# Attention: rotating seven query blocks without a TensorE product

## The chip, the cores and the metric

The kernel runs on one core of a Trainium2 chip. The metric is the device time of one launch in microseconds (us). The kernel before takes 3042.12 us, the median of three runs (3040.42 to 3044.2). TensorE is called PE below, VectorE DVE, ScalarE ACT, GpSimd POOL and SyncE SP, as in the profile.

## The reference

One step of a denoising trunk in four layers, for 128 context tokens and 256 latent tokens of width 1024, all in float32. Each layer is a half-step SwiGLU FFN, a mixer and another FFN. The mixer is attention in layers 0 and 3, a short convolution in layer 1, and a bidirectional gated scan in layer 2. Only attention is touched here. It has 16 query heads and 4 key heads of 64 dimensions. The queries and keys of the 256 latent tokens are rotated (axial rope), those of the context tokens are not:

```python
def apply_rope(x, cos, sin):
    x1, x2 = jnp.split(x, 2, axis=-1)      # 32 + 32 of the 64 dimensions of a head
    c = cos[None, :, None, :]
    s = sin[None, :, None, :]
    return jnp.concatenate([x1 * c - x2 * s, x1 * s + x2 * c], axis=-1).astype(x.dtype)

q = apply_rope(q, cos, sin)
k = apply_rope(k, cos, sin)
...
s_lat = jnp.einsum('bnqkgd,bnskd->bnkgqs', qb, kb) * ATTN_SCALE      # masked window
s_ctx = jnp.einsum('bnqkgd,bskd->bnkgqs', qb, k_ctx) * ATTN_SCALE    # cached keys
p = jax.nn.softmax(jnp.concatenate([s_lat, s_ctx, sink_logits], axis=-1), axis=-1)
o = p_latent @ v + p_ctx @ v_ctx
```

## The kernel before

Everything is one program with an instruction order written out by hand for each engine, and semaphores between the engines. Activations are kept transposed: feature on the partition, the 384 tokens (128 context, 256 latent) along the free axis. A weight block is 128x1024. ACT splits it into a high part `w_hi` (L1876) and DVE makes the low part `w_lo` (L2032); this pair is called split(b). PE multiplies a block in 24 products (`in_block`, L1629 to L1631: high by high, high by low, low by high, for eight slices of the model width) into one PSUM bank.

The attention stage (`pe_attn`, `act_attn`, `dve_attn`, `gp_attn`) projects twelve blocks of 128 outputs: two of keys, two of values, and eight of queries. A query block holds two heads: partitions 0 to 63 and 64 to 127. Within a head, dimension m and dimension m xor 32 form a rotated pair, so rotating a block needs the block itself and a copy in which the four runs of 32 partitions ("quarters") are swapped in pairs: 0 with 1, and 2 with 3. The rotated block is block x cosine + swapped block x sine, with the sine table holding the minus sign for quarters 0 and 2.

The order is `ROPE_ORDER`: key blocks 0 and 1, query block 0, key blocks 2 and 3, then query blocks 1 to 7. The first five (`FIRST_ROPES`) are rotated ahead of the loop. The loop has seven steps, j = 0 to 6. In step j,

- PE: `in_block` of query block j+1 into bank 7; `turn_probs(2j-2)` (L611, seven transposes of the probabilities of a head; `turn_values` instead in step 0); `rotate` (L577), which is the swap, done as a product with a permutation matrix into bank 7 again; `values(j-2)` from step 2 on (L629, L636); `turn_probs(2j-1)` from step 1 on; `scores(j+1)` (L592 to L600) of the block just rotated.
- ACT: `probs(2j)` (L725, L727, the exponentials), `take` (L692, bank 7 to `qkv`), `copy_probs(2j-2)` (L714, L716), `probs(2j+1)`, `output(j-2)` (L732, L733), its part of `copy_probs(2j-1)` (L714), the high part of a split.
- DVE: `maxima(2j)` and `maxima(2j+1)` (L796, L800), `normalize(2j)` (L811, L813 and three instructions at L817), `rope` (L780, swapped block x sine, PSUM to `rope_tmp`; L784, the sum), `split(b0+10+j)` (L2032), `copy_probs(2j-1)` (L806), `normalize(2j+1)`.
- POOL: `cosine` (L859, block x cosine in place), which waits for `rope_rot`, PE's signal behind the rotation; `low_part(j-2)` (L863), which waits for `output(j-2)`.

`scores(j+1)` waits for `rope_add`, the signal of the sum at L784. Behind the loop `out_part` multiplies the outputs by the last eight weight blocks, and the first of these waits for `score_read`, the end of the last maxima. The stage is run twice, in layers 0 and 3.

## Time and profile before

| what | value |
| --- | --- |
| median of three runs | 3042.12 us (3040.42 to 3044.2) |
| profiled execution: its time | 3044.6 us |
| profiled execution: its span | 3042.7 us |
| mean granted TensorE clock | 0.994 |
| PE busy | 2970.3 us (98%) |
| DVE busy | 2210.9 us (73%) |
| ACT busy | 1154.8 us (38%) |
| POOL busy | 588.7 us (19%) |
| the two loops over steps | 372.9 to 440.6 us and 2642.7 to 2710.3 us |

The span is from the first to the last instruction. The time of an execution has 1.9 us more around it. Busy time is the sum over an engine's instructions. An instruction that waits inside for a resource counts as busy, so a duration that is longer than that of its like is a sign of waiting. Rows of the timeline give the start from the beginning of the span, the duration (of several merged instructions: from the first start to the last end), and in brackets the idle time before it and what ended it. Two instructions of one engine can overlap in such rows by some 0.1 us.

### The profile page before, as it was taken

The page shows a single profiled execution, that of the slowest core. Times are in us where ns is not written, and L with a number is a line of the kernel's source. Part 1 is how long each engine was busy: PE and PEld are TensorE (multiplying, and loading weights), DVE is VectorE, ACT ScalarE, POOL GpSimd, SP SyncE. Part 2 cuts the span into 40 slices and gives each one's busy share as a digit, 9 for nine tenths or more (in the row PEclk, how much of TensorE's full clock was granted, in tenths as well). Part 3 has the DMA queues.
Part 4 walks back from the last instruction along what each step waited for, and adds up shares of the span by engine and source line. Part 5 has one row for each costly group of instructions (what it writes and reads, how often), then busy time and mean ns, then how long its engine had stood idle before and what let it go on. Part 6 is the DMA issues. An engine that isn't in the chain of part 4 may idle for free.

```text
span 3042.7 us, 46662 instructions
## 1 busy us (share of the span) xinstructions
PE 2970.3 (98%) x18382; PEld 2753.6 (90%) x18382; DVE 2210.9 (73%) x2845; ACT 1154.8 (38%) x1967; POOL 588.7 (19%) x586
## 2 busy tenths in 40 slices
PE   6999999999999999999999999999999999999999
PEld 6989888999999998999899989979999999889998
DVE  5888687877887566888887576668888888775444
ACT  4222575222422434322422265543224222664222
POOL 1111212112211202112211144441112112211001
PEclk9999999999999999999999999999999999999999
DMA  8676535666566354766566533337664766334443
GB/s 295 200 223 194 144 69 174 209 213 206 167 211 189 105 151 140 235 208 196 184 210 203 149 109 98 98 95 235 208 212 155 222 211 201 113 78 121 125 125 97
DMA packets 565935, 515.59 MB, mean 169 GB/s; under 512 B 43014, under 2 KB 499287, under 8 KB 563927
## 3 DMA queue, kind: packets, MB, share of 16 engines
q1 hardware_dynamic: 565158, 512.37, 55.6%
q8 instruction: 147, 2.41, 0.3%
q14 instruction: 70, 0.57, 0.1%
q10 hardware_dynamic: 560, 0.25, 0.0%
HBM read 509.31 MB, written 3.24 MB: 168 GB/s over the span
## 4 chain that ended last, share of the span: by engine, by line
PE 85%; issue 4%; DVE 4%; DMA 3%; ACT 1%; POOL 1%; SPq 1%; another core or an unknown queue 0%; DVEq 0%; POOLq 0%; ACTq 0%
PE bank L1629 18%; PE bank L1631 18%; PE bank L1630 18%; PE bank L1676 8%; PE bank L1678 8%; PE bank L1677 8%; DMA raw<-w_ffn_in 2%; PE bank L1646 2%; PE bank L1653 1%; DVE fold L2054 1%; PE bank L611 1%; DMA raw<-w_ffn_out 1%; PE bank L636 1%; PE bank L1709 1%; POOL small L2300 0%
## 5 line engine op out<-in xcount | busy, mean ns | idle before, releaser
L1629 PE MATMUL bank<-h_hi,w_hi 128*128 128x384 f32 x3328 | 1122.2, 337 | 6.4 <-DVE tmp L2084 4.1
L1631 PE MATMUL bank<-h_hi,w_lo 128*128 128x384 f32 x3328 | 1115.8, 335 | 0.0
L1630 PE MATMUL bank<-h_lo,w_hi 128*128 128x384 f32 x3328 | 1114.6, 335 | 0.0
L1876 ACT ACTIVATE w_hi<-raw 128x1024 fp32r<-128x1024 f32 x648 | 682.8, 1062 | 1090.6 <-PE bank L1631 443.0
L2032 DVE TENSOR_TENSOR w_lo<-raw,w_hi 128x1024 fp32r<-128x1024 f32 x648 | 812.5, 1276 | 346.7 <-ACT w_hi L1876 340.1
L2054 DVE SCALAR_TENSOR_TENSOR fold<-ada_raw,cond,fold 128x1024 f32<-128x1024 f32 x476 | 654.5, 1432 | 0.0
L1629 PEld LDWEIGHTS bank<-h_hi,w_hi 128*128 128x128 f32 x3328 | 626.2, 188 | 18.2 <-DVE tmp L2084 4.4
L1630 PEld LDWEIGHTS bank<-h_lo,w_hi 128*128 128x128 f32 x3328 | 626.2, 188 | 6.0
L1631 PEld LDWEIGHTS bank<-h_hi,w_lo 128*128 128x128 f32 x3328 | 625.9, 188 | 0.0
L2341 POOL TENSOR_TENSOR h_lo<-tmp,h_hi 128x384 fp32r<-128x384 f32 x176 | 280.5, 1594 | 1762.9 <-DVE h_hi L2088 1762.9
L1676 PE MATMUL bank<-w_hi,h_hi 128*128 128x512 f32 x1056 | 416.2, 394 | 0.0
L1678 PE MATMUL bank<-w_hi,h_lo 128*128 128x512 f32 x1056 | 414.1, 392 | 0.0
L1677 PE MATMUL bank<-w_lo,h_hi 128*128 128x512 f32 x1056 | 413.6, 392 | 0.0
L1895 ACT ACTIVATE tmp<-bank 128x384 f32<-128x384 f32 x176 | 86.3, 490 | 442.7 <-PE bank L1631 437.7
L2084 DVE TENSOR_TENSOR tmp<-bank,tmp 128x384 f32<-128x384 f32 x176 | 97.7, 555 | 212.1 <-PE bank L1631 210.2
L1678 PEld LDWEIGHTS bank<-w_hi,h_lo 128*128 128x128 f32 x1056 | 198.4, 188 | 42.4
L1676 PEld LDWEIGHTS bank<-w_hi,h_hi 128*128 128x128 f32 x1056 | 198.7, 188 | 38.6
L1677 PEld LDWEIGHTS bank<-w_lo,h_hi 128*128 128x128 f32 x1056 | 198.7, 188 | 38.1
L1952 ACT ACTIVATE hf<-bank,mod,s_cols 128x128 f32<-128x128 f32 x288 | 106.5, 466 | 27.2 <-PE bank L1709 26.7
L2126 DVE TENSOR_TENSOR og<-bank,g_rows 128x512 f32<-128x512 f32 x72 | 49.3, 684 | 52.6 <-ACT tmp L1929 52.6
L1676 PE MATMUL bank<-w_hi,o_hi 128*128 128x512 f32 x192 | 77.6, 404 | 1.9 <-DVE soft L796 1.0
L2061 DVE TRANSPOSE_TENSOR_REDUCE fold_sums<-fold 128x64 f32<-128x2048 f32 x34 | 78.3, 2304 | 0.0
(199 smaller groups left out, 2411.6 us busy)
## 6 DMA issues: line engine op xcount, KB each, us to landing
raw<-w_ffn_in SPq DMA_DIRECT2D x352, 512.0 KB, 5.0
ada_raw<-w_ada SPq DMA_DIRECT2D x272, 512.0 KB, 4.2
raw<-w_ffn_out SPq DMA_DIRECT2D x176, 512.0 KB, 4.6
raw<-w_hgrn_in SPq DMA_DIRECT2D x40, 512.0 KB, 3.9
g_rows<-g_dram SPq DMA_DIRECT2D x12, 1024.0 KB, 6.8
raw<-w_attn_qkv SPq DMA_DIRECT2D x24, 512.0 KB, 6.1
raw<-w_conv_in SPq DMA_DIRECT2D x24, 512.0 KB, 5.0
ada_first<-w_ada SPq DMA_DIRECT2D x16, 512.0 KB, 12.3
```

The lines of the kernel that those rows point to most:

```text
L1629: mm(out, wh, h_hi[:, k, :], start=(k == 0), stop=False)
L1630: mm(out, wh, h_lo[:, k, :], start=False, stop=False)
L1631: last = mm(out, wl, h_hi[:, k, :], start=False, stop=(k == DC - 1))
L1676: mm(out, hi[:, tokens(t)], w_hi[:, b % RING, columns(n)], start=opens, stop=False)
L1677: mm(out, hi[:, tokens(t)], w_lo[:, b % RING, columns(n)], start=False, stop=False)
L1678: return mm(out, lo[:, tokens(t)], w_hi[:, b % RING, columns(n)], start=False, stop=closes)
L1876: A(w_hi[:, b % RING, :], raw[:, b % RAW, :], ACT.Copy).then_inc(w_hi_made, 1)
L1952: last = A(hf[:, t, k, :], psum[2 * t + half][:, k % 4 * P:(k % 4 + 1) * P], ACT.Identity, bias=mod[:, 3 * e * DC + k, g:g + 1], scale=s_c ...
L2032: V.tensor_tensor(w_lo[:, b % RING, :], raw[:, b % RAW, :], w_hi[:, b % RING, :].bitcast(F32), ALU.subtract).then_inc(w_lo_made, 1)
L2054: V.scalar_tensor_tensor(out=acc, in0=slab, scalar=c, in1=acc, op0=ALU.mult, op1=ALU.add).then_inc(fold_made, 1)
L2084: V.tensor_tensor(tmp[:, 2 + f % 2, :], psum[7][:, 0:T], tmp[:, f % 2, :], ALU.mult).then_inc(b_read, 1)
L2341: G.tensor_tensor(h2_lo[:, f % H2, :], tmp[:, 2 + f % 2, :], h2_hi[:, f % H2, :].bitcast(F32), ALU.subtract).then_inc(h2_lo_made, 1)
```

## The change

The rotations of query blocks 1 to 7, in the loop, are made without PE. The rotations ahead of the loop stay as they were.

- PE: `rotate` is gone from the steps. PE now also waits, before it overwrites bank 7, for `rope_swapped` of the step before.
- ACT: behind `take`, a new `swap(n)` makes two copies from bank 7 to `rope_tmp`, of 32 partitions and 256 columns each, with a scale of -1: quarter 3 is written to quarter 2, and quarter 2 to quarter 3. It signals `rope_swapped`.
- DVE: `rope` is replaced in the steps by `turned(n)` and `rope_end(n)`. `turned` waits for `rope_swapped` and makes two products with the sine table, again of 32 partitions and 256 columns: bank 7's quarter 1 into quarter 0 of `rope_tmp`, and quarter 0 into quarter 1. Then comes the split, which used to stand behind the sum. Then `rope_end` subtracts `rope_tmp` from the block, 128x256, as soon as the cosine product, both sine products and POOL's sine product are there.
- POOL: `cosine` waits for `qkv_taken` (the end of `take`) in place of `rope_rot`. A new `sine_low` multiplies partitions 64 to 127 of `rope_tmp` by the sine table, in place, once `rope_swapped` and the cosine product are there.
- The counts of `rope_rot` are changed to five for each attention stage.

```diff
--- before.py
+++ after.py
@@ -395,6 +395,7 @@
     ROPE = KVH + DC
 
     attn_in, attn_turned, attn_turn_copied = sem("attn_in"), sem("attn_turned"), sem("attn_turn_copied")
+    rope_swapped, rope_low = sem("rope_swapped"), sem("rope_low")
     rope_rot, k_dup_done, k_dup_copied = sem("rope_rot"), sem("k_dup_done"), sem("k_dup_copied")
     rope_cos, rope_sin, rope_add = sem("rope_cos"), sem("rope_sin"), sem("rope_add")
     sink8_made, score_done, score_read, neg_made = sem("sink8_made"), sem("score_done"), sem("score_read"), sem("neg_made")
@@ -525,6 +526,12 @@
 
         return 6 + n % 2 if n < FIRST_ROPES else 7
 
+    SWAPS = len(ROPE_ORDER) - FIRST_ROPES
+
+    def quarter(q):
+
+        return slice(32 * q, 32 * q + 32)
+
     def rope_dst(n):
         kind, i = ROPE_ORDER[n]
         return kd[:, i, TP:T] if kind == "k" else qkv[:, i, TP:T]
@@ -567,9 +574,7 @@
 
         def rotate(n):
             kind, i = ROPE_ORDER[n]
-            if n >= FIRST_ROPES:
-                pe.wait_ge(qkv_taken, taken + n + 1)
-            elif n >= 2:
+            if n >= 2:
                 pe.wait_ge(rope_sin, ROPE * a + n - 1)
                 if kind == "q":
                     pe.wait_ge(qkv_taken, taken + 3)
@@ -657,13 +662,16 @@
         scores(0)
         for j in range(DC - 1):
 
-            pe.wait_ge(rope_sin, ROPE * a + FIRST_ROPES + j - (1 if j == 0 else 0))
+            if j == 0:
+                pe.wait_ge(rope_sin, ROPE * a + FIRST_ROPES - 1)
+            else:
+                pe.wait_ge(rope_sin, ROPE * a + FIRST_ROPES + j)
+                pe.wait_ge(rope_swapped, SWAPS * a + j)
             in_block(b0 + FIRST_ROPES + j, 7)
             if j == 0:
                 turn_values()
             else:
                 turn_probs(2 * j - 2)
-            rotate(FIRST_ROPES + j)
             if j >= 2:
                 values(j - 2)
             if j >= 1:
@@ -715,6 +723,12 @@
             if h % 2 == 0:
                 A(pt[h % 3][:, 512:KEYS], psum[5][:, 0:KEYS - 512], ACT.Copy).then_inc(pt_copied_v, 1)
 
+        def swap(n):
+            need(act, rope_add, ROPE * a + n - 1)
+            for q in range(2, 4):
+                last = A(rope_tmp[quarter(q), n % 2, :], psum[7][quarter(q ^ 1), TP:T], ACT.Copy, scale=-1.0)
+            last.then_inc(rope_swapped, 1)
+
         def probs(h):
             act.wait_ge(neg_made, HEADS * a + h + 1)
             if h >= 3:
@@ -750,6 +764,7 @@
         for j in range(DC - 1):
             probs(2 * j)
             take(FIRST_ROPES + j)
+            swap(FIRST_ROPES + j)
             if j == 0:
                 copy_values()
             else:
@@ -776,12 +791,27 @@
 
         def rope(n):
 
-            dve.wait_ge(rope_rot, ROPE * a + n + 1)
+            dve.wait_ge(rope_rot, FIRST_ROPES * a + n + 1)
             V.tensor_tensor(rope_tmp[:, n % 2, :], psum[rope_bank(n)][:, 0:TS], sin_t, ALU.mult).then_inc(rope_sin, 1)
 
             dve.wait_ge(rope_cos, ROPE * a + n + 1)
             dve.wait_ge(rope_sin, ROPE * a + n + 1)
             V.tensor_tensor(rope_dst(n), rope_dst(n), rope_tmp[:, n % 2, :], ALU.add).then_inc(rope_add, 1)
+
+        def turned(n):
+
+            dve.wait_ge(rope_swapped, SWAPS * a + n - FIRST_ROPES + 1)
+            for q in range(2):
+                last = V.tensor_tensor(rope_tmp[quarter(q), n % 2, :], psum[7][quarter(q ^ 1), TP:T],
+                                       sin_t[quarter(q ^ 1), :], ALU.mult)
+            last.then_inc(rope_sin, 1)
+
+        def rope_end(n):
+
+            dve.wait_ge(rope_cos, ROPE * a + n + 1)
+            dve.wait_ge(rope_sin, ROPE * a + n + 1)
+            dve.wait_ge(rope_low, SWAPS * a + n - FIRST_ROPES + 1)
+            V.tensor_tensor(rope_dst(n), rope_dst(n), rope_tmp[:, n % 2, :], ALU.subtract).then_inc(rope_add, 1)
 
         def maxima(h):
             n = HEADS * a + h
@@ -831,8 +861,9 @@
             maxima(2 * j)
             maxima(2 * j + 1)
             normalize(2 * j)
-            rope(FIRST_ROPES + j)
+            turned(FIRST_ROPES + j)
             split(b0 + 10 + j)
+            rope_end(FIRST_ROPES + j)
             if j >= 1:
                 copy_probs(2 * j - 1)
             normalize(2 * j + 1)
@@ -853,10 +884,21 @@
         def cosine(n):
             kind, i = ROPE_ORDER[n]
 
-            gp.wait_ge(rope_rot, ROPE * a + n + 1)
+            if n < FIRST_ROPES:
+                gp.wait_ge(rope_rot, FIRST_ROPES * a + n + 1)
+            else:
+                gp.wait_ge(qkv_taken, len(QKV_CHUNKS) * a + n + 1)
             if kind == "k":
                 gp.wait_ge(k_dup_copied, KVH * a + i + 1)
             G.tensor_tensor(rope_dst(n), rope_dst(n), cos_t, ALU.mult).then_inc(rope_cos, 1)
+
+        def sine_low(n):
+
+            gp.wait_ge(rope_swapped, SWAPS * a + n - FIRST_ROPES + 1)
+            gp.wait_ge(rope_cos, ROPE * a + n + 1)
+            low = rope_tmp[HD:P, n % 2, :]
+            G.tensor_tensor(low, low, sin_t[HD:P, :], ALU.mult).then_inc(rope_low, 1)
+            gp.wait_ge(rope_low, SWAPS * a + n - FIRST_ROPES + 1)
 
         def low_part(c):
             gp.wait_ge(mix_hi_made, DC * mi + c + 1)
@@ -870,6 +912,7 @@
         for j in range(DC + 2):
             if j < DC - 1:
                 cosine(FIRST_ROPES + j)
+                sine_low(FIRST_ROPES + j)
             if j >= 2:
                 low_part(j - 2)
```

## Rows read from the trace of the kernel before

**Rows 1.** The page, part 1: busy time, share of the span and instructions.

```profile
PE 2970.3 (98%) x18382; PEld 2753.6 (90%) x18382; DVE 2210.9 (73%) x2845; ACT 1154.8 (38%) x1967; POOL 588.7 (19%) x586
```

**Rows 2.** Busy time of each engine in the second attention stage, by windows.

```profile
2642.00:2716.00 74.00, 71.77 (x620) 64.15 (x618) 63.44 (x210) 52.96 (x153) 10.87 (x13) 1.00 0.27 60
```

**Rows 3.** Timeline of PE: start, duration, engine, line, tiles; in brackets idle before.

```profile
2642.72 0.70 PE L592 MATMUL bank<-kd,qkv 64*128 64x256 f32 x4
...
2651.53 0.70 PE L592 MATMUL bank<-kd,qkv 64*128 64x256 f32 x4 [1.32 <-DVE qkv L784]
...
2660.48 0.70 PE L592 MATMUL bank<-kd,qkv 64*128 64x256 f32 x4
...
2670.45 0.70 PE L592 MATMUL bank<-kd,qkv 64*128 64x256 f32 x4
...
2676.45 0.93 PE L611 MATMUL bank<-base_k,pr 128*128 128x128 f32 x7
2677.22 0.68 PE L577 MATMUL bank<-qkv,attn_k 128*128 128x256 f32 x2
2677.83 0.44 PE L629 MATMUL bank<-pt,vt 128*64 128x128 f32 x4
...
2679.51 0.98 PE L611 MATMUL bank<-base_k,pr 128*128 128x128 f32 x7
2680.42 0.70 PE L592 MATMUL bank<-kd,qkv 64*128 64x256 f32 x4
```

**Rows 4.** Timeline of DVE, from scores(0) to the step of scores(4).

```profile
2644.66 0.62 DVE L796 CUSTOM_DVE_ANT_0 sm<-bank,attn_k,sink 128x384 f32<-128x384 f32 x1 [0.45 <-PE bank L600]
...
2673.14 0.61 DVE L796 CUSTOM_DVE_ANT_0 sm<-bank,attn_k,sink 128x384 f32<-128x384 f32 x1
...
2676.72 0.16 DVE L811 TENSOR_TENSOR soft<-soft 128x3 f32<-128x3 f32 x1 [0.35 <-ACT soft L727]
...
2677.13 0.94 DVE L817 TENSOR_SCALAR pr<-pr,soft 128x384 f32<-128x384 f32 x3
2677.99 0.42 DVE L780 TENSOR_TENSOR rope_tmp<-bank,attn_k 128x256 f32<-128x256 f32 x1
2678.75 0.42 DVE L784 TENSOR_TENSOR qkv<-qkv,rope_tmp 128x256 f32<-128x256 f32 x1 [0.34 <-POOL qkv L859]
2679.09 1.22 DVE L2032 TENSOR_TENSOR w_lo<-raw,w_hi 128x1024 fp32r<-128x1024 f32 x1
2680.53 0.56 DVE L806 COPY pt<-bank 128x384 f32<-128x384 f32 x1 [0.22 <-PE bank L611]
2681.00 1.00 DVE L811 TENSOR_TENSOR soft<-soft 128x3 f32<-128x3 f32 x1
```

**Rows 5.** Timeline of ACT, steps 0 and 3.

```profile
2649.87 0.38 ACT L702 ACTIVATE vt<-bank 128x256 f32<-128x256 f32 x1
...
2676.65 0.49 ACT L692 ACTIVATE qkv<-bank 128x384 f32<-128x384 f32 x1
2677.42 0.60 ACT L714 ACTIVATE pt<-bank 128x512 f32<-128x512 f32 x1 [0.27 <-PE bank L611]
...
2680.42 0.49 ACT L733 ACTIVATE o_hi<-bank 128x384 fp32r<-128x384 f32 x1
```

**Rows 6.** Timeline of POOL, step 3.

```profile
2677.98 0.74 POOL L859 TENSOR_TENSOR qkv<-qkv,attn_k 128x256 f32<-128x256 f32 x1 [5.96 <-PE bank L577]
2680.98 1.00 POOL L863 TENSOR_TENSOR o_lo<-tmp,o_hi 128x384 fp32r<-128x384 f32 x1 [2.27 <-ACT o_hi L733]
```

**Rows 7.** Timeline of DVE before the steps: a split.

```profile
2638.34 1.76 DVE L2032 TENSOR_TENSOR w_lo<-raw,w_hi 128x1024 fp32r<-128x1024 f32 x1
```

**Rows 8.** Timeline of POOL before the steps: a cosine product.

```profile
2638.09 0.92 POOL L859 TENSOR_TENSOR kd<-kd,attn_k 128x256 f32<-128x256 f32 x1
```

**Rows 9.** Timeline of DVE behind the steps: a normalize.

```profile
2717.52 1.77 DVE L817 TENSOR_SCALAR pr<-pr,soft 128x384 f32<-128x384 f32 x3
```

**Rows 10.** Timeline of POOL behind the steps: a low part.

```profile
2717.53 1.02 POOL L863 TENSOR_TENSOR o_lo<-tmp,o_hi 128x384 fp32r<-128x384 f32 x1 [5.63 <-ACT o_hi L733]
```

## The prediction

> **What bounds the kernel now.** I read the page's busy times first: PE is busy for 98% of the span and nothing else comes near [rows 1]. So work taken off PE is worth its time wherever the next engine has room. The windows of an attention stage tell how much room: in 74 us PE is busy for 71.8, but DVE for 63.4 and ACT for 53.0 [rows 2]. DVE is there at 86% of the stage against 73% of the whole kernel. POOL is nearly idle.
>
> Then I read the timeline of the steps. Measured from one start of `scores` to the next, the seven steps take 8.81, 8.95 and five times 9.97 us [rows 3]. Step 3 is the pattern, and I give all its times as offsets from its `scores` at 2670.45. PE has no gap in it: transposes at 6.00, the rotation at 6.77, `values` at 7.38, transposes at 9.06, next `scores` at 9.97 [rows 3]. The rotation holds PE for 7.38 - 6.77 = 0.61 us. Beside it runs a chain: `take` at 6.20 to 6.69 [rows 5], rotation, sine product at 7.54, sum at 8.30 to 8.72 [rows 4]. `scores` needs the sum only at 9.97, so this chain has 1.25 us to spare, less some 0.06 for the signal (in step 0, which has no `values`, PE waits 1.32 us for it [rows 3]). Behind the sum DVE makes its split, from 8.64 on, and the next DVE instruction could start 1.14 us later: 1.22 of duration, less the 0.08 by which the rows of neighbours overlap [rows 4].
>
> **The change, part by part.** *PE.* Seven rotations in each of two stages: 14 x 0.61 = 8.5 us at most, and a full step would last 9.97 - 0.61 = 9.36. The new wait for `rope_swapped` of the step before is long met, since `scores` stands between.
>
> *ACT.* No row shows a copy of 32 partitions. The nearest is the copy of 128x256 from a bank, 0.38 us, 0.26 to its follower's start by my reading of a row's 0.1 us overlap [rows 5]. I take that. The ends are nothing and 0.49 (128x384, [rows 5]). `take` starts at 6.20, the two copies at 6.57 and 6.83, they end at 7.21, and DVE sees it at 7.25. `copy_probs` behind them starts at about 7.09 in place of 6.97 [rows 5], 0.12 late. PE does not notice: it wants that copy at 9.06 less 0.61, and it is made by about 8.1. `output` shifts by the same 0.12, so POOL's low part comes at 10.65 in place of 2680.98 - 2670.45 = 10.53 [rows 6].
>
> *DVE.* The one sine product of 0.42 becomes two, of a quarter of the partitions and the same 256 columns. No row shows such. Ends: nothing and 0.61 (128x384 with a bank, [rows 4]). I take 0.42 each, end to end, 7.25 to 8.09. If they follow at 0.34, as the split follows the sum [rows 4], the second ends at 8.01 and the next can start at 7.93. Then the split, which has changed places with the sum: 8.09 plus 1.14 is 9.23. Then the subtraction, 0.42, as the sum has it: 9.65. With the signal's 0.06, `scores` could start at 9.71, while PE is ready at 9.36. So already without any collision the spare time is used up: the split's 1.14 has been put into a chain with 1.19 to spare, and the second product and the later start take the rest.
>
> The Trainium skill (VectorE: DVE Perf Modes, Two Vector instructions with no wait between them) says that an instruction which starts in another group of 32 partitions than the one before it, for input or output, is held until all earlier ones have finished. No row before shows it. By the rule the products and the split follow at full durations, and by the row at 0.34: the sum below would be 1 to 2 us less by the row.
>
> *POOL.* The cosine no longer waits for PE, so it starts 0.09 behind `take`, at 6.78, in place of 7.53 [rows 6]. `sine_low` has 64 partitions and the cosine's 256 columns. I take the cosine's 0.73 (ends: nothing, and 1.00 for 384 columns [rows 6]). It waits for the cosine's end: 7.59 to 8.32.
>
> *The collision.* A split that is issued while POOL's product runs lasts 1.76 us and not 1.22: it started at 2638.34, POOL's product ended at 2639.01, the split at 2640.10, 1.09 behind that [rows 7, 8]. `normalize` suffers too: with a low part beside it its three instructions took 1.77 us, not 0.94, 0.83 more [rows 4, 9, 10]. So does the small sum at L811, with 1.00 for 0.16 [rows 4, 6]. The sine product from a bank does not: 0.42 with the cosine beside it [rows 4, 6]. So I let a split wait for POOL, and its follower start 1.01 behind POOL's end: 8.32 + 1.01 = 9.33, subtraction to 9.75, `scores` at 9.81.
>
> Steps 0, 1 and 2 come out so, at 9.81: their maxima start 1.94 behind `scores` (step 0, [rows 3, 4]), no low part runs yet, and `normalize(2j)`, which starts 3.99 behind the maxima [rows 4], is over at 6.80. That is +1.00, +0.86 and -0.16 against before.
>
> In steps 3 to 6 the low part, at 10.65, falls 0.84 us into the next step. DVE is then in `normalize` of the odd head, and the maxima start at about 2.4, not 1.94. Before, L811 took the blow and they started at 2.69 [rows 4]. Then `normalize(2j)` runs from 6.39 to 7.25, and the cosine, now at 6.78, falls into its middle. Before, it came at 7.53, behind it. It costs DVE some 0.6 (0.83 for a product of 1.00, scaled to 0.73). The products run from 7.85 to 8.69, the split to 9.83, `scores` starts at 10.31. A step as long as this moves the low part to 0.34 of the next, where it meets either L811 (maxima again at about 2.4) or goes just behind it (at about 2.0, and that step lasts 9.81). I take two in three of the long kind: 10.15, which is +0.18 for each of four steps.
>
> **The sum.** One loop: 1.00 + 0.86 - 0.16 + 4 x 0.18 = 2.4 us. Two loops: 4.8 us. Behind the loop I change nothing. The profiled execution has a span of 3042.7 and a time of 3044.6, so it stands 2.5 us above the median. On its time the sum gives 3049.4, on the median 3046.9, and I forecast 3047. A difference of 0.2%, 6.1 us, is about what a measurement of this kernel can tell from no change, so this is a small loss, just inside it.
>
> **The rivals.**
>
> *No collision costs (20%).* POOL's products slip by DVE or are shorter with 64 partitions. Then steps 0 and 1 end at 9.55 to 9.71, +1.5 for the pair on average, and five steps save 0.42 to 0.26: 1.5 - 1.7 = -0.2 a loop, between -0.8 and +0.4. The time is 3040.5 to 3043. For it: POOL has little to do [rows 2]. Against it: `sine_low` at 7.59 ends where the split begins, by any of my durations.
>
> *Both POOL products cut into `normalize` (16%).* This is the one on the slow side. In steps 3 to 6 DVE's group ends at about 8.75, the split at 10.74, and the low part, due at 10.65, gets in between split and subtraction: `scores` at about 12.1. Such a step leaves the next one clean (9.81), so the mean is 10.95, +0.98 for four steps, 5.6 a loop: 3053. It decides where the maxima start later than about 2.3 and `sine_low` comes before the third instruction of `normalize`.
>
> *PE gets it all back (4%).* That needs the subtraction to end by 9.30, or the products and copies to cost far less on 32 partitions: 3042.1 - 8.5 = 3033.6, less what steps 0 and 1 lose, so some 3036.
>
> *The small instructions are dear (6%).* If each copy takes 0.49 and each product 0.61, a step gets 0.22 + 0.38 = 0.6 longer: 14 x 0.6 = 8.4 on top of 4.8, 3055.
>
> My forecast has 54%.
>
> **How the numbers follow.** My own case reaches from 3044 to 3050. Towards both sides the range takes in the case without collisions (3040.5) and the one in which both products cut in (3053). What is left out is the outer half of the last two rivals and the tails. Faster by over 0.2% (below 3036) is half the third rival and a little of the first: 4%. Slower by over 0.2% (above 3048.2) is 16 + 6, and a fifth of my own case: 33%. Within 0.2%: 63%.
>
> **What would show it.** In the profile after: `scores` about 9.8 us apart in steps 0 and 1 and between 9.8 and 10.4 later; PE waiting for the subtraction ahead of `scores` in each step, 0.4 to 1 us; splits of some 1.4 in the steps; a few `normalize` groups of 1.5; two products of 0.42 behind each other; DVE's busy time up. I am wrong if the rows of 32 partitions are much shorter or longer than those of 128, if `sine_low` ends before DVE's products do, or if the waits of DVE for POOL do not add up along the chain as I let them.

## The result: 0.35% slower

The changed kernel takes 3050.62 us, the median of 8 runs from 3046.66 to 3060.09; the kernel before takes 3040.57 beside it (8 runs, 3037.67 to 3044.98). The ratio is 1.0035, with a 95% interval from 1.0022 to 1.0048, so it is slower by 6.7 to 14.6 us, best 10.6. I had forecast 3047.0 and a range from 3040.5 to 3053.0. The time lies in the range, but it is a loss of more than 0.2%, to which I gave 33%, and it lies just outside my own case of 3044 to 3050. Set on the median that I worked from (3042.12), the ratio gives 3052.8, close to the upper end. The profiled execution took 3051.95 with a span of 3050.1.

The page of the changed kernel, its span and part 1, as in [rows 1]:

```profile
span 3050.1 us, 46690 instructions
...
PE 2965.6 (97%) x18354; PEld 2751.0 (90%) x18354; DVE 2220.9 (73%) x2859; ACT 1165.5 (38%) x1995; POOL 600.9 (20%) x600
```

PE is busy for 4.7 us less, not 8.5. In the seven steps of the first stage, at full clock, it is busy for 62.67 us where it was 65.70; in those of the second it is busy for 67.06 against 65.70, as its products last longer there at a lower clock (below). DVE is busy for 10 more. Then PE's waits in the second attention stage: engine, what it wrote, its line, who released it; total, times, longest.

```profile
PE bank L597 <- DVE qkv L814: 6.3, 6, 3.0
PE bank L616 <- ACT pt L724: 1.7, 1, 1.7
```

Nearly all that PE lost, it lost ahead of `scores`, to the subtraction (L814). One of six waits makes half of the sum. Now the same stage by windows: the 74 us of [rows 2], then step 0, step 1, step 2 and the four steps from 3 to 6 together. Behind each length stand the busy times of PE, PE's weight loads, DVE, ACT and POOL, with the number of instructions; the last three columns are granted clock, DMA share and GB/s.

```profile
2642.00:2716.00 74.00, 66.09 (x516) 59.84 (x516) 61.41 (x197) 51.10 (x146) 14.31 (x18) 0.93 0.27 60
2643.49:2653.51 10.02, 7.05 (x54) 6.58 (x53) 7.79 (x26) 6.73 (x20) 2.17 (x3) 0.96 0.21 65
2653.51:2666.53 13.02, 10.72 (x59) 9.67 (x59) 8.36 (x29) 7.15 (x24) 1.45 (x2) 0.76 0.14 42
2666.53:2678.11 11.58, 11.12 (x87) 9.90 (x87) 8.48 (x30) 7.10 (x22) 1.46 (x2) 0.86 0.15 47
2678.11:2719.19 41.08, 38.17 (x344) 34.84 (x344) 38.46 (x116) 32.45 (x95) 10.42 (x12) 1.00 0.38 58
```

Steps 3 to 6 last 41.08 / 4 = 10.27 each, and step 0 lasts 10.02. Steps 1 and 2 last 13.02 and 11.58, and there the granted clock is 0.76 and 0.86. I had no term for a clock. The other stage shows what these steps are at full clock: its steps last 10.02, 10.00, 10.00, 10.26, 10.26, 10.27 and 10.27, with 1.00 in all. That is 71.08, against 67.63 before, or 3.45 more in a stage; the second stage took 75.70, 4.62 more than the first.

The timeline of PE, second stage, shows what it did before that (start, duration; idle time before in brackets). The rows at the starts of `scores` answer to [rows 3]:

```profile
2653.51 1.23 PE L597 MATMUL bank<-kd,qkv 64*128 64x256 f32 x4 [2.96 <-DVE qkv L814]
...
2664.92 0.96 PE L616 MATMUL bank<-base_k,pr 128*128 128x128 f32 x7 [1.65 <-ACT pt L724]
2666.53 1.22 PE L597 MATMUL bank<-kd,qkv 64*128 64x256 f32 x4 [0.65 <-DVE qkv L814]
...
2678.11 0.70 PE L597 MATMUL bank<-kd,qkv 64*128 64x256 f32 x4 [0.47 <-DVE qkv L814]
```

PE stood still for 2.96 us ahead of `scores(1)`, and the very product that it then issued took 1.23 in place of 0.70. At 2666.53 it is 1.22 again, and at 2678.11 back at 0.70. Before, the idle time there was 1.32 and nothing followed. It is longer by 0.44, by which PE's work in the step now ends earlier, and by 1.21, by which `scores` comes later.

The chain of step 0 on DVE, second stage: products, split, subtraction, as in [rows 4].

```profile
2651.02 0.84 DVE L805 TENSOR_TENSOR rope_tmp<-bank,attn_k 32x256 f32<-32x256 f32 x2 [0.65 <-ACT rope_tmp L729]
2651.89 1.23 DVE L2075 TENSOR_TENSOR w_lo<-raw,w_hi 128x1024 fp32r<-128x1024 f32 x1
2653.03 0.42 DVE L814 TENSOR_TENSOR qkv<-qkv,rope_tmp 128x256 f32<-128x256 f32 x1
```

And of step 3, from `scores` at 2678.11, with the odd head's `normalize` (2678.83) and the even head's (2684.44):

```profile
2678.83 1.70 DVE L847 TENSOR_SCALAR pr<-pr,soft 128x384 f32<-128x384 f32 x3
...
2684.44 1.42 DVE L847 TENSOR_SCALAR pr<-pr,soft 128x384 f32<-128x384 f32 x3
2685.89 0.84 DVE L805 TENSOR_TENSOR rope_tmp<-bank,attn_k 32x256 f32<-32x256 f32 x2
2686.76 1.22 DVE L2075 TENSOR_TENSOR w_lo<-raw,w_hi 128x1024 fp32r<-128x1024 f32 x1
2687.91 0.42 DVE L814 TENSOR_TENSOR qkv<-qkv,rope_tmp 128x256 f32<-128x256 f32 x1
```

ACT's part of step 3 (`take`, then the two copies), as in [rows 5]:

```profile
2684.32 0.49 ACT L700 ACTIVATE qkv<-bank 128x384 f32<-128x384 f32 x1 [0.32 <-PE bank L1674]
2684.83 0.76 ACT L729 ACTIVATE rope_tmp<-bank 32x256 f32<-32x256 f32 x2
```

POOL's `sine_low` of step 0, then its part of step 3 (low part, cosine, `sine_low`), as in [rows 6]:

```profile
2651.14 0.72 POOL L900 TENSOR_TENSOR rope_tmp<-rope_tmp,attn_k 64x256 f32<-64x256 f32 x1
...
2679.24 1.07 POOL L905 TENSOR_TENSOR o_lo<-tmp,o_hi 128x384 fp32r<-128x384 f32 x1 [2.70 <-ACT o_hi L747]
2684.88 0.76 POOL L893 TENSOR_TENSOR qkv<-qkv,attn_k 128x256 f32<-128x256 f32 x1 [4.57 <-ACT qkv L700]
2685.78 0.73 POOL L900 TENSOR_TENSOR rope_tmp<-rope_tmp,attn_k 64x256 f32<-64x256 f32 x1
```

Three things are to be read here. ACT's first copy starts 0.51 behind `take`, when `take` (0.49) is over, and the two copies take 0.76 together. On DVE the split starts 0.87 behind the two products, so these follow at full durations too, and then the subtraction starts 1.14 or 1.15 behind the split, as if POOL were not there: `sine_low` ended before the split began. And both `normalize` groups are longer than 0.94: the odd one 1.70 beside the low part, the even one 1.42 beside the cosine. All four of the steps 3 to 6 have both, in both stages.

### The profile page after: what moved, and what is told of

Its sections match the earlier page's. It is cut to its first block, busy times and chain, and to the rows that moved or that the text cites. A ratio compares the mean times of both kernels' runs of the same rounds, so it can differ in the third digit from the quotient of the medians.

```text
span 3050.1 us, 46690 instructions
## 1 busy us (share of the span) xinstructions
PE 2965.6 (97%) x18354; PEld 2751.0 (90%) x18354; DVE 2220.9 (73%) x2859; ACT 1165.5 (38%) x1995; POOL 600.9 (20%) x600
## 4 chain that ended last, share of the span: by engine, by line
PE 83%; DVE 5%; issue 5%; DMA 3%; ACT 2%; POOL 1%; SPq 1%; DVEq 0%; POOLq 0%; ACTq 0%
PE bank L1672 17%; PE bank L1674 17%; PE bank L1673 17%; PE bank L1719 8%; PE bank L1721 8%; PE bank L1720 8%; DMA raw<-w_ffn_in 2%; PE bank L1689 2%; PE bank L1696 1%; DVE fold L2097 1%; DVE pr L847 1%; DMA raw<-w_ffn_out 1%; PE bank L1752 0%; DVE sm L826 0%; POOL small L2343 0%
## 6 DMA issues: line engine op xcount, KB each, us to landing
ada_first<-w_ada SPq DMA_DIRECT2D x16, 512.0 KB, 12.5
```

## The experiments

The median of the kernel before differs between chips (3039.92, 3041.82, 3048.36 here), so only ratios and steps are compared. For each kernel that was timed, the table sets the time from the first `scores` to the eighth of both stages, less that of before (135.25), beside what the ratio makes of before's median.

| kernel | stages, us | against before | by the ratio (95%) |
|---|---|---|---|
| after | 146.78 | +11.5 | +10.6 (6.7 to 14.6) |
| e1_again | 145.46 | +10.2 | +9.7 (6.4 to 13.4) |
| e2_sum_first | 143.86 | +8.6 | +8.8 (5.2 to 12.5) |
| e3_fill | 143.54 | +8.3 | +9.1 (5.5 to 12.5) |
| e4_cos_late | 162.89 | +27.6 | +23.7 (19.8 to 27.7) |
| e7_b_order | 140.40 | +5.2 | +6.7 (3.7 to 9.8) |
| e8_b_no_rotate | 129.63 | -5.6 | -6.7 (-9.8 to -4.0) |
| e10_hybrid | 138.61 | +3.4 | +2.1 (-0.6 to 4.9) |
| e11_best | 139.64 | +4.4 | +5.2 (2.4 to 7.9) |
| e12_fill_short | 142.43 | +7.2 | +8.5 (5.2 to 11.6) |

In all ten the steps of the one profiled execution alone account for the difference, within the interval. The cause is in the steps and not around them. (The spans themselves can't show this: outside the two stages the profiled executions of these kernels differ by up to 12 us.)

**e1_again.** The changed kernel once more, no edit. Is the slow clock of two steps an accident?

> The changed kernel once more. Two theories share the loss. Chain theory: a fixed part, steps of 10.02, 10.00, 10.00 and four of 10.26 us (67.6 before, 71.1 here), 3.4 us a stage, 6.9 in all, in every execution. Clock theory: on top of it, the 2.96 us for which TensorE idles in step 0 sometimes lets the granted clock fall to 0.5 in step 1 or 2, which cost 4.6 us in one stage of two in the profile. If both hold, the step lengths at clock 1.00 repeat within 0.05 us, the fall shows in some stages and not in others, the times scatter more than before's, and the ratio is 1.003 to 1.004. If the clock has no part, no stage here shows a clock below 1 and both stages last 71.1 us.

Measured: 1.0032 (1.0021 to 1.0044), 3050.69 us. Both stages now have one step at a lower clock, step 1, of 11.60 and 11.62; the other steps are as before it. The windows around `scores(1)` (380.12) of the first stage:

```profile
378.00:380.12 2.12, 0.01 (x1) 0.01 (x1) 2.02 (x4) 2.12 (x8) 0.47 (x1) 1.00 0.00 0
380.12:382.00 1.88, 1.88 (x12) 1.60 (x14) 1.28 (x5) 1.34 (x4) 0.00 (x0) 0.59 0.56 161
382.00:384.00 2.00, 2.00 (x15) 1.77 (x14) 0.81 (x3) 0.00 (x0) 0.00 (x0) 0.53 0.30 119
384.00:386.00 2.00, 2.00 (x14) 2.00 (x13) 1.97 (x10) 1.14 (x5) 0.00 (x0) 1.00 0.00 0
```

PE is busy for 0.01 of 2.12 us, then works nearly without gaps, and is granted 0.59 and 0.53: 2.4 GHz has become 1.2 for most of 4 us, and then comes back. There are eight such stages (after, this kernel, e5 and e6), all with 2.96 us of idle time. In three there was no fall, in three it cost 1.6 us and in two 4.5 or 4.6. The mean is 13.9 / 8 = 1.7 a stage, 3.5 an execution. With 2 x 3.45 = 6.9 from the chain that makes 10.4, though a mean of eight values between 0 and 4.6 is a rough one. One thing I expected is not there: the times scatter over 6.8 us, no more than those of before beside them (6.9).

**e2_sum_first.** The subtraction ahead of the split.

```diff
             turned(FIRST_ROPES + j)
-            split(b0 + 10 + j)
             rope_end(FIRST_ROPES + j)
+            split(b0 + 10 + j)
```

> One thing is undone: the subtraction stands ahead of the split again. Chain theory (the split is what made the sum late): step 0 lasts 8.9 us, step 1 9.3 (ACT's copy of the probabilities is 0.4 later than before), step 2 9.36 (TensorE's own work), steps 3 to 6 9.7 to 9.9 with POOL's products in the middle of normalize; 66.8 a stage against 67.6 before, TensorE idles under 2 us in step 0, so no fall of the clock, and the time is 1 to 3 us under before's, ratio 0.999 to 1.000. Rival (the split costs nothing, it is the small instructions on ACT, DVE and POOL that are dear): steps stay near 10, ratio 1.003.

Measured: 1.0029 (1.0017 to 1.0041), 3051.18 us, where I had expected 0.999 to 1.000: missed. Both stages take 71.93. Step 0 is 8.99, so the split did cost a microsecond there; step 1 is 11.1, at 0.85 of the clock in both stages, behind 1.94 us of idle time, with which I had expected no fall. Steps 3 to 6 are 10.80 and 10.5, where I had expected 9.7 to 9.9. The timeline of DVE and then of POOL in the one whose `scores` start at 2698.50:

```profile
2698.36 1.22 DVE L2075 TENSOR_TENSOR w_lo<-raw,w_hi 128x1024 fp32r<-128x1024 f32 x1
...
2705.55 2.02 DVE L847 TENSOR_SCALAR pr<-pr,soft 128x384 f32<-128x384 f32 x3
...
2708.54 0.43 DVE L814 TENSOR_TENSOR qkv<-qkv,rope_tmp 128x256 f32<-128x256 f32 x1
```

```profile
2705.56 0.73 POOL L893 TENSOR_TENSOR qkv<-qkv,attn_k 128x256 f32<-128x256 f32 x1 [5.12 <-ACT qkv L700]
2706.44 0.73 POOL L900 TENSOR_TENSOR rope_tmp<-rope_tmp,attn_k 64x256 f32<-64x256 f32 x1
```

The split of the step before now stands behind the subtraction, and so ahead of the odd `normalize` and of the maxima. The even `normalize` therefore starts 7.05 behind `scores`, not 6.33. It starts together with the cosine, and `sine_low` gets in ahead of its third instruction: 2.02 us. That is the collision of the "both POOL products" rival, in another kernel than I had put it. What the order gives is taken again by the collision.

**e3_fill and e12_fill_short.** Products on TensorE that nobody reads, in the idle time of steps 0 and 1; in e12 there are 6 and 3 in place of 8 and 6.

```diff
+            if j < 2:
+                pe.wait_ge(rope_sin, ROPE * a + FIRST_ROPES)
+                for _ in range((8, 6)[j]):
+                    mm(psum[6][:, 0:TS], rot_m, cos_t, start=True, stop=True)
```

> The changed kernel with products of 128x256 that nobody reads, eight in step 0 and six in step 1, placed where TensorE idles. They leave the other engines' chain alone. Clock theory: no clock below 1.00 in either stage, steps at 10.0 and 10.3, a stage of 71.1 to 71.5 us in every case, and a time 2 to 4 us under the changed kernel's, ratio to before 1.002 to 1.0025. Rival (the low clock in the one stage was an accident of that execution and not tied to the idle time, or plays no part in the median): the ratio stays at 1.0035 and a low clock shows here too.

> The products that nobody reads again, but six in step 0 and three in step 1 in place of eight and six, which had lengthened these two steps by 0.42 and 0.22 us. Clock theory: the clock stays at 1.00 in both stages, steps 10.02, 10.0, 10.0, 10.27 times four, 71.1 a stage, no stage of 72.7 or 75.7; ratio 1.0023 to 1.0028, under the changed kernel's 1.0033. If the three in step 1 do not suffice, a fall in step 1 or 2 is seen and the ratio stays at 1.003.

Measured: e3 1.0030 (1.0018 to 1.0041), 3049.43 us; e12 1.0028 (1.0017 to 1.0038), 3046.91 us. The granted clock is 1.00 in every step of the four stages. The eight products were too many (step 0 10.44), and e3 missed the 1.002 to 1.0025 that I had expected. With the shorter fill steps 0 to 2 are 10.02, 10.01, 10.00 in one stage, and step 1 is 10.21 in the other. PE ahead of `scores(1)` of e12 (ahead of `scores(2)` it is 0.46 and 0.70 too):

```profile
377.81 0.70 PE L597 MATMUL bank<-kd,qkv 64*128 64x256 f32 x4 [0.37 <-DVE qkv L818]
```

So idle time is what the clock answers to: PE was kept at work, and no fall came in four stages, where five of eight had one. The timed executions say the same by their mean granted clock: 0.9932 in e1, 0.9943 in e3 and 0.9942 in before, all on one chip, and on another 0.9947 in e12 beside 0.9942 in before. The ratios don't separate these kernels from the change (their intervals lie on each other); what is shown is the clock and the steps, 142.43 against 146.78 and 145.46. It also bounds what the clock is worth, since e12, without a fall, is still 0.28% slower than before.

**e4_cos_late.** The cosine waits for the swap, so that it stays out of `normalize`.

```diff
-                gp.wait_ge(qkv_taken, len(QKV_CHUNKS) * a + n + 1)
+                gp.wait_ge(rope_swapped, SWAPS * a + n - FIRST_ROPES + 1)
```

> One wait is changed: POOL's cosine product waits for the swap as well, so it starts some 0.75 us later. Collision theory: it no longer cuts into normalize (that group goes from 1.4 back to 0.94 us), but sine_low now runs to about 9.1 behind scores and holds up the split, which takes 1.8 and not 1.2: steps of 10.5 to 10.6 throughout, 73.5 to 74 a stage, 5 us and more above the changed kernel, ratio 1.005 to 1.006. Rival (no engine holds up the other, the step is set by DVE's own sum of durations): steps stay 10.0 to 10.3.

Measured: 1.0078 (1.0065 to 1.0091), 3064.82 us, the dearest of all. I had expected 1.005 to 1.006 and steps of 10.5 to 10.6: the direction is right, both sizes were missed. Steps are 10.83 at full clock, and 13.6 to 13.7 twice in each stage at 0.75 to 0.78, the first behind 3.77 us of idle time. The timelines of DVE and of POOL in step 4:

```profile
428.56 1.22 DVE L2075 TENSOR_TENSOR w_lo<-raw,w_hi 128x1024 fp32r<-128x1024 f32 x1
430.50 0.42 DVE L814 TENSOR_TENSOR qkv<-qkv,rope_tmp 128x256 f32<-128x256 f32 x1 [0.72 <-POOL rope_tmp L900]
```

```profile
427.73 0.73 POOL L893 TENSOR_TENSOR qkv<-qkv,attn_k 128x256 f32<-128x256 f32 x1 [6.23 <-ACT rope_tmp L729]
428.61 1.76 POOL L900 TENSOR_TENSOR rope_tmp<-rope_tmp,attn_k 64x256 f32<-64x256 f32 x1
```

`normalize` is at 0.95 again. But now the split starts first, at 428.56, and POOL's `sine_low`, issued 0.05 later, lasts 1.76 in place of 0.73. The subtraction needs it and waits 0.72. In the forecast I had DVE wait for POOL; when the split is first, POOL waits for DVE, and the chain pays the same way.

**e5_tiny_cos and e6_tiny_low.** In e5 the cosine of the steps works on 4 of the 256 columns, in e6 `sine_low` does, so most of that product is missing from the result. There is one execution of each, so only the steps are read.

```diff
-            G.tensor_tensor(rope_dst(n), rope_dst(n), cos_t, ALU.mult).then_inc(rope_cos, 1)
+            w = TS if n < FIRST_ROPES else 4
+            G.tensor_tensor(rope_dst(n)[:, 0:w], rope_dst(n)[:, 0:w], cos_t[:, 0:w], ALU.mult).then_inc(rope_cos, 1)
```

```diff
-            low = rope_tmp[HD:P, n % 2, :]
-            G.tensor_tensor(low, low, sin_t[HD:P, :], ALU.mult).then_inc(rope_low, 1)
+            low = rope_tmp[HD:P, n % 2, 0:4]
+            G.tensor_tensor(low, low, sin_t[HD:P, 0:4], ALU.mult).then_inc(rope_low, 1)
```

> The changed kernel, but in the seven steps POOL's cosine product covers 4 of the 256 columns, so most of the block is left without its cosine. Collision theory: nothing cuts into normalize of the even head any more (0.94 us, not 1.42), so steps 3 to 6 fall from 10.27 to about 10.0, the length of step 2; steps 0 to 2 stay at 10.0, where the cosine met nothing. Rival (the cosine's cut is covered and the swap chain alone sets every step): all steps as before this edit, 10.27.

> The changed kernel, but sine_low covers 4 of 256 columns, so half of the swapped block is left without its sine. In the changed kernel sine_low ran beside DVE's two products, which it does not hold up, and ended before the split. So the collision theory expects no change: 10.02, 10.0, 10.0, then 10.27. The rival of the prediction, by which both POOL products cut into normalize or the split, expects steps 0.3 us and more shorter.

Measured: e5 3053.36 us, e6 3052.33 us, where before has 3048.36. In e5 steps 3 to 6 last 10.00 to 10.02 in both stages, not 10.27. In e6 they stay at 10.26 to 10.28, and steps 0 to 2 of the first stage at 10.02, 10.00, 10.00. The timeline of DVE in e5 (even `normalize`, products):

```profile
412.58 0.94 DVE L847 TENSOR_SCALAR pr<-pr,soft 128x384 f32<-128x384 f32 x3
413.79 0.84 DVE L805 TENSOR_TENSOR rope_tmp<-bank,attn_k 32x256 f32<-32x256 f32 x2 [0.26 <-ACT rope_tmp L729]
```

`normalize` is 0.94, and the products now wait 0.26 for ACT's copies. The cosine's collision is worth 0.27 in each of eight steps, 2.1 us, and the chain from `take` alone gives 10.0. `sine_low` costs nothing in the changed kernel's order.

**e7_b_order.** The kernel before, with PE's rotation, and only the split put ahead of the sum.

```diff
+            if n >= FIRST_ROPES:
+                split(b0 + 5 + n)
             dve.wait_ge(rope_cos, ROPE * a + n + 1)
...
-            split(b0 + 10 + j)
```

> The kernel before, with only the split put ahead of the sum. Chain theory: steps 0 and 1 lose all of it, 9.8 us each for 8.81 and 8.95 (the split starts beside POOL's cosine and takes 1.7 us), steps 2 to 6 have 1.19 us to spare and stay at 9.97; 69.4 a stage for 67.6, plus up to 1.6 us more where the clock falls after TensorE's 2.3 us of idle time in step 0. Ratio 1.001 to 1.002. Rival (the order does not matter, the small instructions do): steps as before, ratio 1.000.

Measured: 1.0022 (1.0012 to 1.0032), 3053.9 us on a chip where before has 3048.36. Steps are 9.78, 9.72 and 9.97 to 10.00 in the first stage. PE ahead of `scores(1)` (0.73 ahead of `scores(2)`):

```profile
381.18 0.70 PE L592 MATMUL bank<-kd,qkv 64*128 64x256 f32 x4 [2.28 <-DVE qkv L786]
```

The order by itself costs 0.97 and 0.77 in steps 0 and 1 and nothing behind them, where PE is the limit at 9.97. In the second stage step 1 was 11.36, at 0.85, behind the same 2.28 us of idle time.

**e8_b_no_rotate.** The other bound: the kernel before with the rotation of the steps left out and nothing in its place, so the swap is missing from the result. The sine product and the cosine wait for `take`, as the cosine does in the changed kernel.

```diff
-            rotate(FIRST_ROPES + j)
...
+            src = psum[rope_bank(n)][:, 0:TS] if n < FIRST_ROPES else psum[7][:, TP:T]
+            V.tensor_tensor(rope_tmp[:, n % 2, :], src, sin_t, ALU.mult).then_inc(rope_sin, 1)
```

> The kernel before without the seven rotations in the steps: the sine product reads the block itself from the bank, so the swap is left out of the computation and costs nothing. It shows what TensorE's 0.61 us is worth at most. If TensorE is the bound, steps 2 to 6 last 9.36. If DVE's own round is as long (8.2 us of its instructions, 0.36 waiting for the exponentials, 0.85 held up by the low part, and now 0.6 by the cosine, which comes early), they last 9.8 to 10.0 and the saving is worth next to nothing. I expect the second; step 0 gets shorter (8.0 to 8.2), step 1 stays at 8.95 (ACT's copy).

Measured: 0.9978 (0.9968 to 0.9987), 3042.09 us against 3048.36. Steps 8.03, 9.20 and 9.45 to 9.60, clock 1.00. I had expected 9.8 to 10.0 in steps 2 to 6, so this missed. A free swap is worth 2.8 a stage, 5.6 us, of the 8.5 that the rotations take. The window of step 3, a part of PE's timeline in it, and PE's wait in step 1:

```profile
396.87:406.32 9.45, 9.45 (x87) 8.70 (x86) 8.78 (x29) 7.21 (x23) 1.73 (x2) 1.00 0.19 55
```

```profile
402.87 0.93 PE L611 MATMUL bank<-base_k,pr 128*128 128x128 f32 x7
403.73 0.44 PE L629 MATMUL bank<-pt,vt 128*64 128x128 f32 x4
```

```profile
386.26 0.95 PE L611 MATMUL bank<-base_k,pr 128*128 128x128 f32 x7 [1.11 <-ACT pt L717]
```

PE is busy for all of steps 2, 3 and 5, of 9.48, 9.45 and 9.50, so its bound is some 9.45 to 9.5 and not 9.36: `values` starts 0.86 behind the transposes, where the rotation started 0.77 behind them [rows 3]. Leaving the rotation out is worth some 0.5 a step and not the 0.61 for which it holds PE. The largest part of the rest is lost in step 1, which is longer than before (9.20 for 8.96): PE waits there 1.11 us for ACT's copy of the probabilities, where it waited 0.60 before. In the later steps DVE holds PE up by 0.07 at most, though the early cosine makes an even `normalize` last 1.48 (step 4).

**e9_no_cross.** No crossing of partitions: one copy and one product of 64 partitions, each read from where it writes, so the swap is missing from the result. There is one execution.

```diff
-            for q in range(2, 4):
-                last = A(rope_tmp[quarter(q), n % 2, :], psum[7][quarter(q ^ 1), TP:T], ACT.Copy, scale=-1.0)
+            last = A(rope_tmp[HD:P, n % 2, :], psum[7][HD:P, TP:T], ACT.Copy, scale=-1.0)
...
-            for q in range(2):
-                last = V.tensor_tensor(rope_tmp[quarter(q), n % 2, :], psum[7][quarter(q ^ 1), TP:T],
-                                       sin_t[quarter(q ^ 1), :], ALU.mult)
+            last = V.tensor_tensor(rope_tmp[0:HD, n % 2, :], psum[7][0:HD, TP:T], sin_t[0:HD, :], ALU.mult)
```

> The changed kernel with the crossing left out: ACT makes one copy of partitions 64 to 127 onto themselves and DVE one product of partitions 0 to 63 onto themselves, so the swap is missing from the result. It prices the four crossing instructions. Theory: an instruction that starts on other partitions than the last waits for the end of the last, on ACT as on DVE: 0.51 from take to the first copy, 0.38 and 0.42 end to end. With one of each, without crossing, the copy ends 0.5 us earlier and the product takes half. POOL then becomes the last to finish: sine_low waits behind the split, steps 0 to 2 last 9.7 and steps 3 to 6 last 9.9, against 10.0 and 10.27. Rival (a short instruction costs the same wherever it reads and writes, and the wait for normalize sets the start): steps within 0.1 of the changed kernel's.

Measured: 3046.38 us, before 3039.92 there. Steps 9.90, then 9.9 and 10.41 in turn, step 1 at 0.85 of the clock. I had expected 9.7 and then 9.9: missed by 0.2 and by the long kind. The timelines of ACT, DVE and POOL:

```profile
405.30 0.49 ACT L700 ACTIVATE qkv<-bank 128x384 f32<-128x384 f32 x1 [0.34 <-PE bank L1671]
405.81 0.38 ACT L728 ACTIVATE rope_tmp<-bank 64x256 f32<-64x256 f32 x1
```

```profile
406.74 0.41 DVE L803 TENSOR_TENSOR rope_tmp<-bank,attn_k 64x256 f32<-64x256 f32 x1
407.07 1.20 DVE L2072 TENSOR_TENSOR w_lo<-raw,w_hi 128x1024 fp32r<-128x1024 f32 x1
```

```profile
406.74 2.12 POOL L897 TENSOR_TENSOR rope_tmp<-rope_tmp,attn_k 64x256 f32<-64x256 f32 x1
```

The product on DVE's usual partitions lets the split follow at 0.33, so crossing costs DVE 0.1 for each instruction. The copy still starts 0.51 behind `take`: it begins at partition 64, `take` at 0. And the step hardly gains, since `sine_low` and the split meet again and `sine_low` pays. In the steps of 9.9 the split starts about 0.2 ahead and `sine_low` lasts 1.6. In those of 10.41, shown here, `sine_low` starts 0.33 ahead of the split and still lasts 2.12, while the split keeps its 1.20.

**e10_hybrid.** The change in steps 2 to 6 only; steps 0 and 1 keep PE's rotation and the old order.

```diff
+            if j < 2:
+                rotate(FIRST_ROPES + j)
...
-            turned(FIRST_ROPES + j)
-            split(b0 + 10 + j)
-            rope_end(FIRST_ROPES + j)
+            if j < 2:
+                rope(FIRST_ROPES + j)
+                split(b0 + 10 + j)
+            else:
+                turned(FIRST_ROPES + j)
+                split(b0 + 10 + j)
+                rope_end(FIRST_ROPES + j)
```

> Steps 0 and 1 keep TensorE's rotation and the old order, steps 2 to 6 have the change. Chain theory: 8.81, 8.95, then 10.0 and four of 10.26, 68.8 a stage against 67.6 before. TensorE idles 1.3 us at most, so the clock stays at 1.00 in both stages and the times scatter like before's. Ratio 1.0008. Of the 3.4 us a stage the two first steps carried 2.3. Rival (the clock falls here too, or the loss sits in the later steps): ratio 1.002 or more.

Measured: 1.0007 (0.9998 to 1.0016), 3041.28 us: not to be told from before. Steps 8.82, 8.94, 10.49 and 10.26, clock 1.00. I had expected 10.0 in step 2, which missed: its even `normalize` lasts 1.42 already, with the cosine in it. PE at the starts of `scores(1)` and `scores(3)`:

```profile
375.60 0.70 PE L600 MATMUL bank<-kd,qkv 64*128 64x256 f32 x4 [1.33 <-DVE qkv L806]
...
395.03 0.70 PE L600 MATMUL bank<-kd,qkv 64*128 64x256 f32 x4 [0.95 <-DVE qkv L821]
```

The idle time ahead of `scores(1)` is 1.33 again and the clock stays up. Of the 5.2 us that a stage lost on average (3.45 by the chain, 1.7 by the clock) 1.7 are left: two thirds came through steps 0 and 1.

**e11_best.** e10, with the subtraction ahead of the split in steps 2 to 6, and a cosine that waits for the even `normalize`.

```diff
+                gp.wait_ge(p_normed, HEADS * a + 2 * (n - FIRST_ROPES) + 1)
...
                 turned(FIRST_ROPES + j)
-                split(b0 + 10 + j)
                 rope_end(FIRST_ROPES + j)
+                split(b0 + 10 + j)
```

> The same, and in steps 2 to 6 the subtraction stands ahead of the split and POOL's cosine waits for the end of normalize of the even head, so that it cuts into nothing but DVE's products, which do not mind. It is the version that the theories point to. Step 2 at 9.4 to 9.5, steps 3 to 6 at 10.0 to 10.1: DVE's own round, 8.2 us plus 0.5 for the second product, 0.36 waiting for the exponentials and 0.85 for the low part, is then the bound. 67.4 a stage, ratio 1.000, so the change is worth nothing even at its best. If DVE's round is not the bound, steps 3 to 6 last 9.4 to 9.6 and the ratio is 0.9985.

Measured: 1.0017 (1.0008 to 1.0026), 3043.71 us: slower than e10. A stage takes 69.82, and steps 3 to 6 about 10.5; I had expected 67.4 and 10.0 to 10.1. The timelines of DVE and POOL in a step:

```profile
413.15 0.95 DVE L854 TENSOR_SCALAR pr<-pr,soft 128x384 f32<-128x384 f32 x3
...
415.97 0.43 DVE L821 TENSOR_TENSOR qkv<-qkv,rope_tmp 128x256 f32<-128x256 f32 x1 [1.00 <-POOL rope_tmp L912]
```

```profile
414.24 0.72 POOL L905 TENSOR_TENSOR qkv<-qkv,attn_k 128x256 f32<-128x256 f32 x1 [6.20 <-DVE pr L854]
415.11 0.73 POOL L912 TENSOR_TENSOR rope_tmp<-rope_tmp,attn_k 64x256 f32<-64x256 f32 x1
```

No `normalize` (0.95) and no split (1.22) is cut into any more, and the sum of POOL's two products is what remains: they don't start before 414.24, and the subtraction waits 1.00 for the second. The swap gives POOL two instructions in a row on the path, and in steps 3 to 6 I found no place for them that costs nothing. No version that I tried and that does the swap beats the kernel before.

## Why it went so

*The stage is bound by PE, and the rotation is worth 0.61 a step.* Right that PE is the bound, but the limit is some 9.45 to 9.5 and not 9.36 (e8, and e2's step 2 with PE busy for all of its 9.46), so a rotation is worth some 0.5. Of the 8.5 us only 5.6 were to be had, and what stands in the rotation's place, with the split ahead of the subtraction, costs 71.08 - 64.82 = 6.3 a stage.

*ACT.* The price was too low. I took a spacing of 0.37 and then 0.26 + 0.38; it was 0.51 and 0.76. The swap ends at about 7.47 for 7.21, 0.26 late. The copies follow at full duration, as if behind each other's end; I had read the overlap from neighbours that start on the same partitions.

*DVE's two products.* Right: 0.84 for 0.84, each a full 0.42. The Trainium skill (VectorE: DVE Perf Modes, Two Vector instructions with no wait between them) says that an instruction which starts in another group of 32 partitions is held until the earlier ones are over. The trace agrees for DVE: 0.87 from the first product to the split here, 0.33 from an uncrossed one in e9. The page speaks of Vector only; ACT's copies behave alike here.

*The split against `sine_low`.* Wrong in the changed kernel. The later products put the split behind `sine_low` (2651.89 against an end at 2651.86 in step 0), and it ran its 1.23 undisturbed. This is a sign of being wrong that I had named: `sine_low` ends with DVE's products in step 0 and 0.22 ahead of their end in step 3. Without the collision my sum for such a step is 9.71, the products start 0.28 later than I had them and last 0.03 longer to the split: 10.02 for 9.81. e4 and e9 show the collision, and there POOL pays and not DVE: 1.76 where the split starts 0.05 ahead, 2.12 where `sine_low` starts 0.33 ahead. In [rows 7, 8] POOL's product started 0.25 ahead and the split paid. So the recorded starts alone don't tell who pays, and that stays open.

*The cosine in `normalize(2j)`.* Right. I had the group at 6.39 and 0.6 longer; it came at 6.33 and was 0.48 longer, and the step was 10.27 where I had 10.31 for the long kind. e5 takes it away and gets 10.0. The mixture was wrong: I let two steps in three be long, and all four are, as the low part meets the odd `normalize` (1.70) in each of them.

*The sum.* Steps 0 to 2 cost 1.21 + 1.04 + 0.03 = 2.3 a stage (forecast 1.7), the others 4 x 0.29 = 1.2 (forecast 0.7). Twice this is 6.9, and I had 4.8. With 6.9 alone the time would be 3047.5, a hair over the mark of 0.2%. My sum is less than half of the measured 10.6. That the time still lies in the range is in part luck: the upper end was there for a rival that did not happen, and a term that I did not have filled the room.

*The term that was missing.* The other 3.5 us, the mean of the eight profiled stages, are TensorE's clock. I said that PE would wait 0.4 to 1 us in each step, and did not add it up in step 0, where there are no `values`: 2.96. The Trainium skill (TensorE: Matmul & The Clock Gate, Part 1) says that the chip gates PE's clock by how busy it has lately been; the trace agrees, by a granted clock of 0.53 behind that gap in e1 and of 1.00 in e12, where it is filled. A fall does not come each time. The granted clock of the timed executions supports the size: e1 has 0.0010 less than before, and 0.0010 of 3050 us is 3 us, an estimate. The times alone don't show it, since the intervals of e3 and e12 lie on that of the change. Nor does the scatter: the changed kernel scatters over 13.4 us, its slowest execution at 0.990 and its fastest at 0.995, but e1 over 6.8 and e3, with PE kept at work, over 10.8.

*The rivals.* "No collision costs" was right on the split and `sine_low`, and fell with e5 for the cosine. "Both POOL products cut in" did not happen in the changed kernel, though its 3053 was the nearest figure, nearer than my own 3047: a number alone would have confirmed the wrong mechanism. e2 shows its collision. "The small instructions are dear" fell with durations of 0.38 and 0.42; only that ACT's copies don't overlap goes its way. "PE gets it all back" is refuted by the result, and e8 shows how much even a free swap gives: 5.6 to 6.7 us, about what that rival asked for.

What stays open is also why the clock falls in some stages and not in others with the same idle time. A kernel before with only an early cosine was not tried, since PE's rotation still reads that block.

## What to carry to other kernels

Work taken off the busiest engine is worth nothing where it lengthens the chain that this engine waits for, so find the steps in which the chain has no cover (here 0 and 1, ahead of `values`) and leave these as they are: that alone took the loss from 0.35% to 0.07%, which is not to be told from none. Add up the idle time that a change leaves on TensorE at one place: behind 1.9 to 3.8 us in a row the clock fell in 12 stages of 16 here, and took half as much again as the chain did. Instructions of a quarter of the partitions were not cheaper here than those of all, and lost the overlap with their neighbours; and moving a POOL product earlier is an edit to whatever DVE does with SBUF at that time.

## What the runs showed of the hardware

- A copy of 32x256 from a bank on ACT takes 0.38 us, as one of 128x256 does [rows 5]; a product of 32x256 on DVE 0.42, as one of 128x256 [rows 4]; one of 64x256 on POOL 0.73, as one of 128x256 [rows 6]. In these pairs the columns are the same, and the number of partitions made no difference.
- ACT's copies that start on another partition than the one before them began when that one was over: 0.51 behind a `take` of 0.49, with 32 partitions (after) and with 64 (e9), and two of 0.38 took 0.76. Neighbours on the same partitions overlap by some 0.1. No run changed the partition alone.
- The wait between DVE and POOL works both ways, and between two instructions of a group: `normalize` took 0.94, 1.42, 1.70 or 2.02 by what of POOL fell in it, and POOL's `sine_low` 0.73, 1.6, 1.76 or 2.12 where the split fell in it. A product that reads a bank was untouched.
- Granted clock: idle times of 1.9 to 3.8 us ahead of `scores(1)` were followed in 12 of 16 stages by some 3 to 7 us at a granted clock near 0.5, sometimes twice, at a cost of some 1.6 to 5.7 us. In the four stages of e3 and e12, with that time filled, and in the eight of before, e8, e10 and e11, where PE never waited for more than 1.33 us at once, the clock stayed at 1.00.
